# Down projection, fourth norm and gated embedding of a two-block layer put into one interleaved phase

## The reference

```
x  = x + act @ w_down                        # 2816 -> 1024
xn = x * rsqrt(mean(x*x) + 1e-6) * ple_norm_g   # the fourth norm
out = x + sigmoid(xn @ w_ple_gate) * (p @ w_ple_proj)   # 1024 -> 1024, 256 -> 1024
```

## Time and profile before

| | us |
|---|---|
| median of 3 runs (3029.92 to 3040.23) | 3032.33 |
| the profiled execution | 3038.24 |
| its span, first to last instruction | 3036.5 |
| TensorE busy in the span | 2648.6 (87%) |
| VectorE, ScalarE, GpSimd busy | 1271.9, 955.2, 260.2 |
| mean granted TensorE clock | 0.936 of full |

### The profile page before, as it was taken

How to read it: one execution, slowest core, us unless ns; L and a number is a source line. 1 busy time by engine, 2 the same in 40 slices (tenths; PEclk the granted TensorE clock), 3 DMA queues, 4 the chain that set the end, 5 groups by cost and what they waited for, 6 DMA issues and landing times. The chain is left out here.

```text
span 3036.5 us, 38505 instructions
## 1 busy us (share of the span) xinstructions
PE 2648.6 (87%) x15182; PEld 2287.0 (75%) x15182; DVE 1271.9 (42%) x1815; ACT 955.2 (31%) x1547; POOL 260.2 (9%) x351
## 2 busy tenths in 40 slices
PE   5979999995998946799975888799999998999569
PEld 4859999995887835688874767678888886778469
DVE  4433444433555534443136757354333332333332
ACT  3323322212455532123115666433111111222321
POOL 0002222211000000001002222010000000000000
PEclk9979999997999977899987999999999999999779
DMA  2322222103321133342243111153221210454432
GB/s 91 111 76 77 65 59 58 53 29 90 86 68 49 42 110 126 128 146 79 88 155 108 44 39 36 59 177 94 66 84 63 75 57 35 148 180 145 149 104 91
DMA packets 229770, 268.82 MB, mean 89 GB/s; under 512 B 55236, under 2 KB 167492, under 8 KB 229608
## 3 DMA queue, kind: packets, MB, share of 16 engines
q1 hardware_dynamic: 228552, 264.48, 27.3%
q10 hardware_dynamic: 1056, 2.10, 0.2%
HBM read 189.30 MB, written 77.22 MB: 88 GB/s over the span
## 5 line engine op out<-in xcount | busy, mean ns | idle before, releaser
L3712 PE MATMUL ffn_up_acc<-mixed_hi,ffn_ring_hi 128*128 128x512 f32 x704 | 274.1, 389 | 2.6 <-DVE mixed_lo L3115 2.5
L3712 PE MATMUL ffn_up_acc<-mixed_hi,ffn_ring_lo 128*128 128x512 f32 x704 | 273.9, 389 | 0.0
L3712 PE MATMUL ffn_up_acc<-mixed_lo,ffn_ring_hi 128*128 128x512 f32 x704 | 273.9, 389 | 0.0
L1717 PE MATMUL delta_acc<-delta_w_hi,xn_hi 128*128 128x256 f32 x640 | 192.0, 300 | 2.9 <-DVE delta_w_lo L1671 2.9
L1719 PE MATMUL delta_acc<-delta_w_hi,xn_lo 128*128 128x256 f32 x640 | 181.5, 284 | 0.0
L1718 PE MATMUL delta_acc<-delta_w_lo,xn_hi 128*128 128x256 f32 x640 | 181.4, 283 | 0.0
L2894 PE MATMUL trunk_acc<-trunk_ring_hi,merged_hi 128*128 128x512 f32 (+1 forms) x384 | 149.4, 389 | 17.3 <-DVE trunk_ring_lo L2852 17.3
L2008 PE MATMUL ffn_down_acc<-ffn_down_hi 128*128 128x512 f32 x352 | 139.7, 397 | 25.9 <-DVE ffn_down_lo L1993 25.9
L3712 PEld LDWEIGHTS ffn_up_acc<-mixed_hi,ffn_ring_hi 128*128 128x128 f32 x704 | 132.1, 188 | 30.4 <-issue 3.0
L3712 PEld LDWEIGHTS ffn_up_acc<-mixed_hi,ffn_ring_lo 128*128 128x128 f32 x704 | 132.1, 188 | 27.5
L3712 PEld LDWEIGHTS ffn_up_acc<-mixed_lo,ffn_ring_hi 128*128 128x128 f32 x704 | 132.1, 188 | 27.3
(11 more groups left out here) (412 smaller groups left out, 6299.7 us busy)
## 6 DMA issues: line engine op xcount, KB each, us to landing
ffn_down_raw<-scratch_act_t SPq DMA_DIRECT2D x44, 512.0 KB, 3.5
ffn_ring_raw<-in_w_gate SPq DMA_DIRECT2D x11, 1024.0 KB, 5.3
ffn_ring_raw<-in_w_up SPq DMA_DIRECT2D x11, 1024.0 KB, 5.8
scratch_act_t<-ffn_silu SPq DMA_DIRECT2D x22, 512.0 KB, 2.6
ffn_down_raw<-in_w_down SPq DMA_DIRECT2D x44, 256.0 KB, 3.7
delta_w_raw<-in_w_in SPq DMA_DIRECT2D x20, 512.0 KB, 4.0
scratch_projected<-delta_out SPq DMA_DIRECT2D x80, 128.0 KB, 1.7
stick_g_raw<-in_w_in SPq DMA_DIRECT2D x16, 512.0 KB, 4.5
```

What stands on the lines that cost most here:

```text
L1717: nc.tensor.matmul(acc, self.hi[:, k, tok], w_hi, start=(k == 0), stop=False, skip_group_check=True)
L3712: last = nc.tensor.matmul(self.acc[s][:, br, cols], weight[:, k, ch], part[:, k, cols], start=(k == 0 and first), stop=(k == 7 and weight ...
```

## The change

The five parts become one phase, "tail", in which eight stages are interleaved by `tail_plan`. The PSUM is four pairs of banks. Two views of it are lent to other stages: `turn` (pairs 0 and 1, for transposes) and `acc` (the four banks of pairs 2 and 3).

- `Embedding`: loads `p` and `w_ple_proj`, turns and splits them, makes p @ w_proj in 16 units of 512 columns (6 products each) ahead of all else, and stores them to a new scratch tensor `emb`.
- `Feed`: per step 128 features: 512 tokens of `act_t` and all 1024 columns of `w_down`, again 128 x 1536 to split in two slots, 22 steps for each of two groups of four token tiles.
- `Down`: per step 4 token tiles x 3 products x 2 halves; the 22nd step is cut into four, one token tile each. VectorE adds the residual in place, 1024 columns, so `x` stays in SBUF.
- `TailSquare`, `TailScale`, `TailTurn`: the norm, one token tile at a time; the inverse root by two small operations and a power on GpSimd. The first four tiles' squares and two of their scalings stand between the steps of the second group.
- `GateWeights`: `w_ple_gate` in four pieces of 128 x 2048, two of them in the second group, two after it.
- `GatedEmbedding`: 16 units of 512 columns (24 products each), sigmoid, product with the stored embedding unit read back, sum with `x`, store.

```diff
-        ffn_down(nc, "ffn_down", act_t, a["w_down_2"], x2, x3)
-            norm_to_features(nc, "norm4", x3, [a["ple_norm_g_2"]], hi[:, 0:8], lo[:, 0:8], ident)
-            turn_features(nc, "embedding", a["p_2"], hi, lo, 8, ident)
-            project_embedding(nc, "ple", hi, lo, a["w_ple_gate_2"], a["w_ple_proj_2"], x3, out)
+        with Phase(nc, "tail") as ph:
+            pairs = [ph.ps(f"pair{j}", [P, 2, HALF]) for j in range(4)]
+            turn = Lent(ph, "turn", [pair[:].rearrange("p h (k t) -> p (h k) t", t=P) for pair in pairs[0:2]])
+            acc = Lent(ph, "acc", [pair[:, half, :] for pair in pairs[2:4] for half in range(2)])
...
+def tail_plan(n):
+    emb, feed, down, square, scale, turn, gates, ple = range(8)
+    plan = [emb, feed, emb, feed] + [emb] * 16
+    for i in range(n - 1):
+        plan += [down, feed]
+    plan += [down] * 4 + [feed]
+    for i in range(n - 1):
+        plan += [down]
+        plan += [feed] * (i < n - 2)
+        plan += [square] * (2 <= i < 6)
+        plan += [scale] * (i in (4, 6))
+        plan += [gates] * (i in (2, 8, 12))
+    plan += [down, down, down, turn, down, turn, scale, square, square]
+    plan += [square, square, ple, turn, gates, scale]
+    plan += [ple, turn, scale]
+    plan += [ple, turn, gates, scale]
+    plan += [ple, turn, scale]
+    plan += [ple, turn, scale]
+    plan += [ple, turn]
+    plan += [ple] * 10
...
+class Down:
+    def tensor(self, pe):
+        for i, tiles in self.walk():
+            s, first = i % 2, i % f.n == 0
+            if tiles[0] == 0:
+                pe.wait_ge(f.lo_done[s], i // 2 + 1)
+            for j in tiles:
+                if first and i == 0:
+                    self.embedding.release(pe, j)
+                elif first:
+                    pe.wait_ge(t.added, j + 1)
...
+class TailTurn:
+    def tensor(self, pe):
+        for m in range(TT):
+            key = ("norm", m)
+            t.turn.wait_free(pe, key)
+            if m < 2:
+                pe.wait_ge(t.added, Tail.JOINT + m + 1)
+            pe.wait_ge(t.scaled, m + 1)
+            for k in range(8):
+                last = t.nc.tensor.transpose(t.turn.tile(key)[:, k, :], t.xn[m % 2][:, k * P:(k + 1) * P], t.c["ident"][:])
...
+class GatedEmbedding:
+    def units(self):
+        return [(c, 4 * g + j) for g in range(2) for c in range(2) for j in range(4)]
+    def tensor(self, pe):
+        for u, (c, m) in enumerate(self.units()):
+            t.acc.wait_free(pe, key)
+            if u < 4:
+                pe.wait_ge(t.added, Tail.JOINT + 3 + u // 2)
+            if c == 0:
+                t.turn.wait_read(pe, ("norm", m))
+            if m == 0:
+                pe.wait_ge(w.lo_done, 2 * c + 2)
```

More of the change, by code:

```diff
@@ L1927, in _ @@
                 slot_loop(pe, n, step)
[L1931 to L2022, removed]
@@ new lines, with __init__, takes, walk @@
+class Down:
+    def __init__(self, t, feed, embedding):
+        self.t, self.feed, self.embedding = t, feed, embedding
+    def takes(self, at):
+        return []
+    def walk(self):
+        f, every = self.feed, range(Tail.JOINT)
+        return [step for i in range(2 * f.n) for step in ([(i, [j]) for j in every] if f.last(i) else [(i, every)])]
+    def sync(self, sp):
+        t = self.t
+        for step, (i, tiles) in enumerate(self.walk()):
+            if 4 <= step < 4 + 2 * TT and step % 2 == 0:
+                m = (step - 4) // 2
+                sp.dma_start(t.x[:, m, :], t.residual[tile_of(m), :]).then_inc(t.x_in[m], 16)
+            if step == 3:
+                sp.dma_start(t.gain_row[:], row(t.gain)).then_inc(t.gain_in, 16)
+            yield
+    def gpsimd(self, pool):
+        return iter(())
+    def scalar(self, act):
+        return iter(())
+    def vector(self, dve):
+        t, f = self.t, self.feed
+        for i, tiles in self.walk():
+            if f.last(i):
+                m = i // f.n * Tail.JOINT + tiles[0]
+                dve.wait_ge(f.summed, m + 1)
+                dve.wait_ge(t.x_in[m], 16)
+                x = t.x[:, m, :]
+                t.nc.vector.tensor_tensor(x, x, t.pairs[tiles[0]][:].rearrange("p h n -> p (h n)"), ALU.add).then_inc(t.added, 1)
+            yield
+    def tensor(self, pe):
+        t, f, nc = self.t, self.feed, self.t.nc
+        for i, tiles in self.walk():
+            s, first = i % 2, i % f.n == 0
[6 more added lines that the diff above has]
+                    pe.wait_ge(t.added, j + 1)
+                hi, lo = f.hi[s][:, j * P:(j + 1) * P], f.lo[s][:, j * P:(j + 1) * P]
+                for part, weight, begins, ends in ((hi, f.hi[s], first, False), (hi, f.lo[s], False, False),
+                                                   (lo, f.hi[s], False, f.last(i))):
+                    for half in range(2):
+                        last = nc.tensor.matmul(t.pairs[j][:, half, :], part, weight[:, HALF + half * HALF:HALF + (half + 1) * HALF],
+                                                start=begins, stop=ends, skip_group_check=True)
+            last.then_inc(f.summed if f.last(i) else f.used[s], 1)
+            yield
@@ new lines, in tail_plan @@
+def tail_plan(n):
[18 more added lines that the diff above has]
+    plan += [ple] * 10
+    return plan
```

525 lines of the change are left out of this document (383 added, 142 removed).

## The result

The changed kernel takes 2957.8 us (median of 4 runs, 2950.9 to 2961.1) where the kernel before took 3035.6 beside it: a ratio of 0.974, 95% interval 0.9715 to 0.9768. The forecast was 2955.8, the range 2944 to 2981. The profiled execution has a span of 2957.1 us.

The account below looks back on a forecast made before the run. TensorE's product starts bound the tail, 106.7 of 469.7 us not being products. Border, embedding, down, gate, turns, waits and end summed to a span of 2960.0 against 3036.5; 76.5 off the 3032.3 median gave 2955.8 us, range 2944 to 2981.

Parts of the forecast that it names:

- The phase border: Start of the tail: loads in by 2584.9, then splits, first embedding product at 2590.5; bounds 2588 and 2594.
- The embedding: 96 products ahead of the down steps: 21.8 us, 3 for the low clock, 1 for late stores.
- The down steps: Down projection: 1056 products in 239.4 us instead of 252.2, with no waits in steps or between groups.
- The holes: TensorE's waits after the last down group, chiefly 4.4 us before turn 3: 5.9 us in sum, bounds 0 and 12.
- The gate and the end: 384 gate products 87.1 us, eight turns 6.3 us; last product to last instruction 5.0 us, bounds 4.3 and 7.
- The clock: TensorE's clock across a 4.4 us wait: no fall taken; bounds none and two falls, 3 us each.
- My premise: Idle of 2.6 us in the phase ahead left the clock at 1.00; 6.7 us did not.
- The price of width: Embedding and gate: 512 columns take 0.2267 us, 256 take 0.120; wide products cost 108.9 us against 115.2.
- A: More waits stay: longer chain after the last group, two clock falls, stores holding embedding units; about 2975 us, chance 0.22.
- B: Fewer waits stay: loads land sooner and late tile waits cost nothing; 2947 us, chance 0.13.
- C: Down steps: the feed becomes the bound if landing takes over 6.8 us; at 11 us, 3047 us; chance 0.03.
- D: Groups not joined, as engines wait in plan order; 2995 us with half the 76.6 us stretch back; chance 0.04.

Follow-up runs that it names:

- new front: Changed kernel with p turned and split ahead of the projection's weights, these split in two column halves; tail 391.1 us against 391.3 to 391.4.
- Experiment 3: Changed kernel with the splits of the second group's first two feature tiles put behind the first group's residual adds; 2961.3 us.
- experiment 6: Changed kernel with each feature tile's down weights loaded a second time into a spare buffer that nothing reads; 2958.2 us.
- experiment 2: Changed kernel with squares, scalings, turns and gate weight splits all planned between the last down step and the first gate unit; 2986.6 us.
- new order: Changed kernel with the next tile's scaling ahead of the gate weights' split in VectorE's queue at two places; tail 388.7 us, 2.7 less.
- experiment 4: Kernel with the second group's first two splits behind the residual adds, plus one unused VectorE sum behind the fourth add; tail 397.4 us.
- experiment 1: Changed kernel with each of the 384 gate products of 512 columns made as two of 256; 2962.3 us.

## Why the prediction was right, and where its terms were off

The forecast tail, 2960.0 - 2566.8 = 393.2 us by its own sum, measured 391.0. Term by term:

*The phase border.* First embedding product expected 2590.5 - 2566.8 = 23.7 us after the last up product, measured 23.8. The projection's weights were in by 2584.4, against my 2584.9 from the same number of bytes in the earlier trace rows.

*The embedding.* 25.8 expected, 24.1 measured (2589.9 to 2614.0). The low clock cost 2.3 us and not 3 in this profile (2.3 to 3.1 over the nine with the same start), and the stores nothing, where I had 1. The mechanism that I named for that 1 us is there, as the kernel with the new front shows; it lay just under the surface.

*The down steps.* 239.4 expected. Measured 241.9 with two turns (1.6 to 1.8) and a wait of 0.5, which leaves 239.6 to 239.8. No step waited, also not where squares, scalings and weight pieces stand in the queues, and the border of the groups shows no gap. Experiment 3 prices the border at 3.2 us, and experiment 6 shows that the feed has room; what it is worth to have the squares and scalings in the second group is priced only together with the whole order, in experiment 2.

*The holes.* 5.9 us expected, 3.3 measured: 0.5, 1.8 and 1.1 where I had 0.3, 4.4 and 1.2. (The new order, which removes the last two, gives back 3.2 us for their 2.8, so each also delays what stands behind it a little.) The step that failed is the length of a square. I took 0.63 + 0.19 for each half, 1.64 for a tile, the square and the readout of its sum one after the other. In the trace after, the next square starts 0.61 to 0.62 us behind the last, since the readout runs into the next one's start:

```profile
2856.85 0.62 ACT L3964 ACTIVATE tail_gate<-tail_x 128x512 f32<-128x512 f32 x1
2857.37 0.19 ACT L3964 ACTIVATION_READ_ACCUMULATOR tail_gate<-tail_x 128x1 f32 x1
2857.46 0.62 ACT L3964 ACTIVATE tail_gate<-tail_x 128x512 f32<-128x512 f32 x1
```

Four tiles take 4.9 us in place of the 6.7 in my chain, and the first sigmoid is read that much earlier. On my time scale VectorE's scaling of tile 3 ends at 21.6 in place of 23.7, and TensorE comes to the turn at 19.9 in place of 19.3: that is how 4.4 became 1.8. The chain itself was right: the hole before the turn of tile 3 was ended by VectorE's scaling, with the weight piece's subtraction before it, and it went when the two changed places (the new order).

*The gate and the end.* 87.1 + 6 turns: 95.8 measured with 2.8 of holes, so 93.0 for 384 products and six turns, which leaves a turn at 0.98 and not at 0.79. In the kernel with the new order, where no holes stand in it, the same stretch is 92.6 and a turn 0.92. My row measured up to the next product's start, and the product behind it comes late too (0.31 us behind it in place of 0.227, at 2862.1 in the trace after). From the last product to the last instruction it is 5.5 us; I had 5.0.

*The clock.* I took no fall, and none came, but this was luck. The hole of 4.4 us that I expected had shrunk to 1.8, and the one hole of nearly that length on record, 4.2 us in experiment 4, ended the full clock. My premise doesn't hold either. The 2.6 us of idle in the earlier trace rows are mostly one idle of 2.5 us at 2096.2 to 2098.7, 1.3 us ahead of that row's end, and the same idle ended the full clock in six of thirteen profiles. So a hole of 1.8 us isn't safe by what these runs show. The bound that I gave (3 us a fall) covered the prices measured, 1.6 to 2.9.

*The price of width.* I went by the rows against the Trainium skill (TensorE: Matmul & The Clock Gate, Back-to-back issue gap), where the wider form saves 1 us. The trace doesn't agree with that page here: 256 columns take 0.120 us in the kernel before and in experiment 1, 512 take 0.2267 in before and after, and the gate alone is 5.1 us by that, of which experiment 1 bears out 4.8 to 5.2 once the shorter holes are counted.

So the sum was right to 2 us with errors of both signs: the holes 2.6 too high and the embedding 1.7 too high, the turns and the end some 2 too low. That they nearly cancel is luck. In the median the forecast is 2.0 us too low although the gain was larger than forecast (77.7 against 76.5), since the kernel before took 3.2 us more beside it (3035.6 against 3032.3). Of the rivals, A has one true part (the embedding's stores do hold units back once the start is earlier), B was the nearest miss, C and D were not seen.

## What to carry to other kernels

Where the matrix engine idles at phase borders, count two gains apart: what stays when the phases are joined but run in sequence, and what the order inside hides. Here they were 52 us (most of it a shorter way from the last down product to the first gate product, then the break between the halves and its slow restart) and 27. Lay the instructions of the last, uncovered stretch out by hand over all queues, with the distance of two starts and not the printed durations as their length. And before shortening a start, look for the chain that lies just behind it: here it took 2.1 and 1.2 us of waiting in two profiles, and none once its buffer was doubled. Where a difference of 1 us matters, take out of the comparison the stretches that start at the lower clock, since the same instructions there differed by 0.8 us between profiles.

## What the runs showed of the hardware that was not expected

The length of an idle doesn't decide alone whether TensorE's full clock is kept. It was lost after an idle of 2.1 us in one profile and outlasted 3.0 us in another, and the same idle of 2.5 us, between the same instructions, ended it in six of thirteen profiles. Where it fell after 2.1, 2.5 and 4.2 us, seven or eight products of 512 columns ran at 1.2 GHz (1.6 us), after 5.5 us fourteen (2.8 us); the start of the embedding, the same code each time, had ten to thirteen.

ScalarE's readout of a running sum, 0.19 us in the trace, costs nothing between two squares of 512 columns: the second starts 0.61 us after the first, as long as one square's own 0.62. In experiment 2 the step from one tile to the next is 0.73 us in the last four tiles, which no run explains.

With the down weights loaded twice (278 GB/s against 184, DMA engines at 79%), the first of the two loads landed 0.2 us later in the median, the features' 256 KB 0.2 us and the gate weights' 1 MB 1.5 us later.
